# One-hot operands of the gate matrices stored in groups of two tokens instead of four

## The reference, cut to what matters

```
q = (xi @ w_q).reshape(n, 8, 2, 128)
s = einsum('nhpc,hpkc->nhpk', q, sub_keys)          # 128 scores per head and side
ts, ti = top_k(s, 16)                               # the 16 best of each side
best_s, best_p = top_k(pair sums of both sides, 16) # the 16 best pairs
idx  = a * 128 + b                                  # expert = key a, key b
gate = softmax(best_s)
act  = gelu(einsum('nd,nhkd->nhk', xi, u[idx]))
y    = einsum('nhk,nhkd->nd', gate * act, v[idx])
```

## Time and profile before

| | |
|---|---|
| median of three runs | 2338.49 us (2335.31 to 2339.03) |
| the profiled execution, first to last instruction | 2339.2 us |
| its TensorE busy | 2182.7 us, 93% |
| its VectorE busy | 1528.4 us, 65% |
| its ScalarE busy | 897.1 us, 38% |
| its GpSimd busy | 729.7 us, 31% |
| the stretch of the gate matrices | 921 to 1126 us of the span |

### The profile page before, as it was taken

How to read it: one execution, slowest core, us unless ns; L and a number is a source line. 1 busy time by engine, 2 the same in 40 slices (tenths; PEclk the granted TensorE clock), 3 DMA queues, 4 the chain that set the end, 5 groups by cost and what they waited for, 6 DMA issues and landing times.

```text
span 2339.2 us, 31291 instructions
## 1 busy us (share of the span) xinstructions
PE 2182.7 (93%) x12743; PEld 1269.1 (54%) x12743; DVE 1528.4 (65%) x2558; ACT 897.1 (38%) x1066; POOL 729.7 (31%) x540
## 2 busy tenths in 40 slices
PE   6999889998999988999999999999879998999998
PEld 5464554444665555777656555555545455444444
DVE  4557763248979999999578888888767174433002
ACT  5333552333343324566433333333232354444110
POOL 2311001312414242222133343343417401544540
PEclk9999989998999999999999999999979999999999
DMA  5223552225877776877899999999722211233310
GB/s 200 73 73 141 183 181 72 91 73 193 320 251 289 276 284 227 324 285 286 321 356 376 377 380 381 378 379 380 250 101 73 101 49 37 73 108 108 144 36 36
DMA packets 194479, 483.39 MB, mean 207 GB/s; under 512 B 10672, under 2 KB 93648, under 8 KB 188320
## 3 DMA queue, kind: packets, MB, share of 16 engines
q1 hardware_dynamic: 154624, 334.65, 40.3%
q0 software_dynamic: 39712, 146.74, 16.6%
HBM read 428.92 MB, written 52.43 MB: 206 GB/s over the span
## 4 chain that ended last, share of the span: by engine, by line
PE 53%; DVE 24%; DMA 15%; ACT 3%; issue 3%; POOL 1%; SPq 1%; DVEq 0%; ACTq 0%; POOLq 0%
PE psum L559 14%; PE psum L560 14%; PE psum L561 14%; DMA expert_act<-act_dram 12%; DVE weight_low L1988 6%; DVE row_sum L2217 2%; PE psum L961 2%; DMA rows_b<-peer_v_dram,row_index 2%; POOL weight_low L2538 1%; DVE hidden_low L2384 1%; PE psum L753 1%; DVE expert_act L2379 1%; DVE rows_a L2204 1%; DVE rows_b L2204 1%; PE psum L844 1%
## 5 line engine op out<-in xcount | busy, mean ns | idle before, releaser
L559 PE MATMUL psum<-x_high,weight_high 128*128 128x384 bf16 (+3 forms) x1856 | 650.5, 350 | 37.6 <-DVE weight_low L1988 23.3
L560 PE MATMUL psum<-x_low,weight_high 128*128 128x384 bf16 (+3 forms) x1856 | 649.1, 350 | 0.0
L561 PE MATMUL psum<-x_high,weight_low 128*128 128x384 bf16 (+3 forms) x1856 | 648.5, 349 | 0.0
L1275 ACT ACTIVATE weight_high<-weight_stage 128x4096 bf16<-128x4096 f32 (+2 forms) x100 | 356.2, 3562 | 237.6 <-PE psum L561 119.2
L2538 POOL TENSOR_TENSOR weight_low<-weight_stage,weight_high 128x512 bf16<-128x512 f32 (+1 forms) x229 | 300.0, 1345 | 428.1 <-ACT weight_high L1275 428.0
L559 PE MATMUL psum<-hidden_high,weight_high 128*128 128x384 bf16 x1024 | 334.9, 327 | 10.7 <-DVE hidden_low L2384 10.7
L560 PE MATMUL psum<-hidden_low,weight_high 128*128 128x384 bf16 x1024 | 334.9, 327 | 0.0
L561 PE MATMUL psum<-hidden_high,weight_low 128*128 128x384 bf16 x1024 | 334.8, 327 | 0.0
L1988 DVE TENSOR_TENSOR weight_low<-weight_stage,weight_high 128x4096 bf16<-128x4096 f32 x69 | 304.8, 4418 | 35.8 <-ACT weight_high L1275 35.8
L559 PEld LDWEIGHTS psum<-x_high,weight_high 128*128 128x128 bf16 (+1 forms) x1856 | 185.9, 100 | 201.6 <-DVE weight_low L1988 27.6
L561 PEld LDWEIGHTS psum<-x_high,weight_low 128*128 128x128 bf16 (+1 forms) x1856 | 185.5, 100 | 158.0 <-issue 12.1
(11 more groups left out here) (350 smaller groups left out, 2983.1 us busy)
## 6 DMA issues: line engine op xcount, KB each, us to landing
weight_stage<-peer_u_dram SPq DMA_DIRECT2D x32, 2048.0 KB, 8.6
weight_stage<-peer_v_dram SPq DMA_DIRECT2D x32, 2048.0 KB, 11.7
weight_stage<-mlp_w_dram SPq DMA_DIRECT2D x16, 2048.0 KB, 8.0
weight_stage<-ada_w_dram SPq DMA_DIRECT2D x12, 2048.0 KB, 8.0
act_dram<-norm_value SPq DMA_DIRECT2D x128, 192.0 KB, 9.9
gate_dram<-gate_matrices SPq DMA_DIRECT2D x12, 2048.0 KB, 12.0
gates<-gate_dram SPq DMA_DIRECT2D x32, 768.0 KB, 16.9
expert_act<-act_dram SPq DMA_DIRECT2D x32, 768.0 KB, 18.6
```

The source lines that it names most:

```text
L559: self.nc.tensor.matmul(out, left[0], right[0], start=first, stop=False)
L560: self.nc.tensor.matmul(out, left[0], right[1], start=False, stop=False)
L561: return self.nc.tensor.matmul(out, left[1], right[0], start=False, stop=last)
L1275: nc.scalar.activation(k.block_view(m.w_high, n % SPLITS, n), k.block_view(m.w_stage, n % STAGES, n), ACT.Copy).then_inc(*s.w_high.up(n))
```

## The change

`OI`, the number of tokens that lie innermost in the one-hot arrays, goes from 4 to 2. The arrays keep their size: instead of 2 groups of 128 keys x 4 tokens they hold 4 groups of 128 keys x 2 tokens. For TensorE the elements of one token now lie 2 bf16 elements (4 bytes) apart and not 4 (8 bytes). For VectorE the picks' numbers and gates, which are repeated over the 128 keys, are now read in runs of 2 elements and not of 4. The helper array `m.iota` shrinks from 512 to 256 elements. The index of a token is worked out with `divmod`, as a group of PSUM still holds four tokens. No instruction is added, removed or moved on any engine.

```diff
-OC, OI = 8, 4
+OC, OI = 8, 2
...
                 for x in range(4):
                     for part in range(2):
-                        ins = nc.tensor.matmul(k.psum[:, i, NK * x:NK * (x + 1)], m.left[:, v, q, :, x],
-                                               m.gated[part][:, v, q, :, x], start=part == 0, stop=part == 1)
+                        c, y = divmod(4 * q + x, OI)
+                        ins = nc.tensor.matmul(k.psum[:, i, NK * x:NK * (x + 1)], m.left[:, v, c, :, y],
+                                               m.gated[part][:, v, c, :, y], start=part == 0, stop=part == 1)
```

## The result

The changed kernel takes 2326.28 us (median of five runs, 2322.58 to 2327.79) against 2338.49 us (five runs, 2335.12 to 2342.22). The ratio is 0.9946, 95% interval 0.9932 to 0.9960: faster by 0.54%, 12.6 us. It ran again in the last experiment (e12), at 0.9944 (0.9931 to 0.9957). The profiled execution has a span of 2323.5 us, 15.7 us less than the profiled one of before; it is one execution each, so the ratio of the runs is what counts.

The account below looks back on a forecast made before the run. In the gate matrices TensorE and VectorE, both nearly full, alternate on the chain. Gains of 6.7 to 10.3 us in the stage and 0.7 to 1.9 at its end, taken as 9, gave 2339.2 - 9 = 2330.2, said as 2330 us, range 2326 to 2343.

Parts of the forecast that it names:

- The pace of the one-hot matmuls: TensorE in the gate matrices: 118.8 ns a matmul falls to between 58 and 98 ns.
- rival A: The forecast itself: one-hot matmul pace falls below about 100 ns, VectorE becomes the stage's only bound, 2330 us; chance 0.47.
- VectorE's arrays unchanged: VectorE's four arrays a step in the gate matrices stay at 685 ns each; nothing in the forecast.
- Rival D: VectorE's arrays pay for short runs: 392 or 539 ns more each, 2404 or 2432 us; chance 0.12.
- the third add: VectorE's 256-element add of line 2320, pairs 32 bytes apart: 393 ns, not 294, read as 1.8 ns a pair.
- VectorE becomes the only bound: Gate matrices: VectorE's 10.3 us wait goes to near zero, TensorE's rises from 12.9 to 30 us or more.
- The sum: Gate-matrix stage and its end together gain 7.4 to 12.2 us; 9 us taken, allowing for TensorE's lower clock.
- The upper sum: Best end for the gate matrices: VectorE's 10.3 us idle time plus 1.9 us behind its last array, 12.2 us.
- The gain arrives: Behind the gate matrices: the DMA-bound stretch starts as much earlier as the stage ends earlier; nothing subtracted.
- B: One-hot matmuls on TensorE: pace only falls from 118.8 to 112 ns, 2336.8 us; chance 0.17.
- C: One-hot matmuls on TensorE: nothing changes, the step isn't what makes the loads slow, 2339 us; chance 0.17.
- E: TensorE waits longer, so each period has a second stretch at 1.2 GHz on the path, 8 us, 2338; chance 0.05.

Follow-up runs that it names:

- e12: The changed kernel itself, run again on the same chip: 2325.95 us, ratio 0.9944 to the kernel before.
- e1: Kernel before with two tokens innermost only in the moving operand (one_hot_b and gated arrays), the stationary one keeping four: 2328.35 us, ratio 0.9942.
- e5: Changed kernel without the low part of the gate, three VectorE arrays a step instead of four, TensorE's work kept: 2305.41 us, ratio 0.9863 to the kernel before.
- e10: Changed kernel with 24 gathered rows in the gate matrices instead of 36, twelve moved behind the stage: 2323.62 us, ratio 0.9930 to the kernel before.
- e3: Changed kernel with eight tokens innermost instead of two, 16 bytes between one token's elements: 2462.60 us, ratio 1.0516 to the kernel before.
- e6: Kernel before (four tokens innermost) without the low part of the gate, three VectorE arrays a step, TensorE's work kept: 2318.41 us, ratio 0.9916.
- e2: Kernel before with two tokens innermost only in the stationary operand one_hot_a, the moving arrays keeping four: 2339.39 us, ratio 1.0000.

## Why the prediction was right or wrong

- **The pace of the one-hot matmuls.** Forecast 58 to 98 ns from 118.8, with 58 from VectorE's 1.8 ns per 16 bytes; measured 57.5 from 117.2. The number taken over from VectorE held at 8 and 16 bytes. Why it did is not shown: VectorE's 1.8 ns were measured with 32 bytes from place to place, TensorE's with 8 and 16, and the 16 bytes in between were an assumption that nothing here has tested apart from others, so there may be luck in it. The upper end, 98 ns "if loads don't overlap each other", was wrong, since the record of a load is not its price (e1). The scatter of the load records, which rival A counted for itself, is no sign either: in the changed kernel it is wider, 96 to 149 ns, at the pace of contiguous reads.
- **VectorE's arrays unchanged.** 685 ns forecast, 685 to 693 measured. Rival D is out: runs of exactly two elements cost nothing when the place does not change. So the 1.8 ns of the third add are not the price of a short run, and its distance of 32 bytes is what is left. (If pairs had been lost, an array would have taken 1227 - 685 = 542 ns more, not the 539 of the prediction.)
- **VectorE becomes the only bound.** Its wait of 10.3 us went entirely, TensorE's rose to 37.0 us (forecast: 30 or more). "Only" is too strong, by e5 and by e10, where the next bound showed at once.
- **The sum, the step that failed.** The mechanism was right and a term was mis-sized. The terms gave 7.4 to 12.2 us and I took 9, "because a TensorE that waits more falls to its lower clock more often". It did: the granted clock fell from 0.93 to 0.89 in the stage. But a stretch at the lower clock lay on the chain six times before (at 942, 976, 1010, 1044, 1078 and 1112 us) and twice after (1068.59 and 1100.36), and the first of these two held VectorE up by 0.04 us at most. With VectorE as the bound, a slow stretch of TensorE eats its waits, and only the one at the end of the stage counts, which was there before too. So nothing was to be deducted, and the low end, 7.4, rested on the 98 ns that the bursts disprove.
- **What the runs showed in its place.** The upper sum was 10.3 + 1.9 = 12.2 us. What the traces show in its place is 10.8 us between VectorE's first array and its last, and 2.3 us behind the last array, together the 13.0 us by which the stage is shorter. The runs, with 9.4 to 15.9 us, can't tell 12.2 from 13.0, but they exclude 8.5.
- **The range** was the second fault: it ended 1 us below the sum's own best end, 2339.2 - 12.2 = 2327.0, and that is less than the runs scatter, so whether the result fell just inside or just outside was chance.
- **The gain arrives.** The DMA-bound sums behind the stage kept their share (0.99) and began sooner; nothing was given back. The profiled execution gained 15.7 us: 13.0 in the stage, 1.0 ahead of it and 1.7 behind, and the last two are within what single executions differ by.
- **The rivals.** B (one word at a time) would have had 112 ns for both 4 and 8 bytes, and C no change: the burst rules out both. E's mechanism was there without its effect, as said above.
- **What the rivals cite.** Rival C rests in part on the rule of the Trainium skill ("SBUF — State Buffer", Door 1: The DMA port swizzle) that a step of up to 8 bf16 elements is free. This case does not agree: 4 elements already doubled the price and 8 (e3) quadrupled it; only 2 were free. The 16-byte lines that the Trainium skill gives there fit the prices, but 32 bytes would too (see the table of the four widths). What rival D takes from the Trainium skill ("Vector Engine (DVE) Microarchitecture Reference", 5.1) is said there of two elements per partition in all, not of runs of two within 1024; that such runs go in pairs is shown here by the 685 ns.

## What to carry to other kernels

A moving operand read with a step made the matmul dearer here: nothing to speak of at 4 bytes between elements (57.5 ns for 128 columns against 56.1 contiguous), twice the price at 8 and four times at 16. Some 1.8 ns for each 16 bytes touched sums this up for the steps that were run. A step of 8 bytes in the stationary operand added only 1.8 ns (59.3 against 57.5, e1). At TensorE's lower clock there was little to win: 118 ns became 105. Where a layout serves two engines, take the narrowest group that the second engine still handles at full rate (two bf16 elements for VectorE), since all beyond it was paid by the first. And when one of two engines that take turns gets faster, the gain here was the other's wait plus the tail behind its last instruction (10.8 + 2.3 us); slow-downs of the faster engine inside its new idle time are not to be deducted.

## What the runs showed of the hardware that I had not expected

- A TensorE that is busy all the time can still fall to its lower clock: with 233 ns per 128 columns the granted clock was 0.74 at 323.00 of 323.00 us busy (e3), while at 117 ns, equally busy, it was 0.98 (e6). It cost some 51 us.
- The recorded duration of a weight load says little of its price: 113 ns at a pace of 59 ns (e1), and 117 ns for a load whose operand was finely packed, in a burst whose stream was slow (e2).
- With 8 bytes between the elements a matmul of 128 columns took 117 to 118 ns at either clock (bursts of 2.06 us for 16 and 3.93 us for 32), where with 4 bytes it took 105 ns at the lower clock and 57.5 at the full one. So the price of the step is one in ns, not in TensorE's clock periods.
- VectorE and TensorE show the same number, 1.8 ns, for a new place, VectorE with 32 bytes from one to the next and TensorE with 8 and 16 (as two and one elements to 16 bytes), though their own rates differ (1.035 ns a pair, 0.44 ns a column). Whether they have one cause is open.
